# Four of the seven PSUM banks held over the second norm are copied to SBUF in an encoder layer on eight cores

## The reference, cut to what matters

```python
def conv_ffn(x, conv_prev, g_pre, w_up, w_conv, b_conv, w_down, g_post):
    h = rms_norm(x, g_pre)
    gate, val = jnp.split(h @ w_up, 2, axis=-1)          # (B, T, 5632) each
    ext = jnp.concatenate([conv_prev, gate], axis=1)     # two earlier rows in front
    conv = b_conv + sum(ext[:, i:i + T] * w_conv[i] for i in range(3))
    y = (jax.nn.silu(conv) * val) @ w_down
    return rms_norm(y, g_post), ext[:, T:]
```

## Time and profile before

| | us |
|---|---|
| median of 3 runs | 6721.76 |
| lowest and highest run | 6713.4 and 7092.37 |
| the profiled execution's own time | 6715.98 |
| its span on the slowest core (core 4) | 6714.9 |
| spans of the eight cores | 6661.3 to 6714.9 |
| mean granted TensorE clock, core 4 | 0.967 of full |
| TensorE busy | 6102.4 |
| VectorE busy | 2672.6 |
| ScalarE busy | 1740.5 |
| GpSimd busy | 314.4 |

### The profile page before, as it was taken

The page is one execution under the profiler, slowest core; times in us unless marked ns, Lnnn a source line. Parts: engine busy times, 40 slices in busy tenths (PEclk is TensorE's granted clock), DMA queues, the critical chain, the costliest instruction groups (busy, mean ns, idle before and its releaser), DMA issues.

```text
span 6714.9 us, 91958 instructions; the slowest of 8 cores (6661.3 to 6714.9 us)
## 1 busy us (share of the span) xinstructions
PE 6102.4 (91%) x33070; PEld 3235.3 (48%) x33412; DVE 2672.6 (40%) x4680; ACT 1740.5 (26%) x2772; POOL 314.4 (5%) x1160
## 2 busy tenths in 40 slices
PE   6879899898999999899967999899989989998997
PEld 3434345343454445444444455555656565554443
DVE  3343233433334433353333543443444335433532
ACT  2222113221133212331122321321332233223310
POOL 1011000010000000000000100000000000000000
PEclk9989999999999999999988999999999999999999
DMA  9979983899737796444564456457556745754443
GB/s 199 212 152 184 192 218 107 197 207 220 226 120 213 208 244 202 148 163 158 196 217 160 179 197 218 167 205 238 194 186 207 254 159 205 244 197 152 163 158 137
DMA packets 214673, 1276.44 MB, mean 190 GB/s; under 512 B 24192, under 2 KB 45584, under 8 KB 86992
## 3 DMA queue, kind: packets, MB, share of 16 engines
q1 hardware_dynamic: 175376, 1008.93, 43.4%
q0 software_dynamic: 37184, 257.79, 20.7%
q10 hardware_dynamic: 1664, 3.81, 0.2%
HBM read 1275.76 MB, written 184.30 MB: 217 GB/s over the span
## 4 chain that ended last, share of the span: by engine, by line
PE 72%; DMA 15%; DVE 6%; ACT 3%; issue 3%; SPq 0%; DVEq 0%; POOL 0%; ACTq 0%; POOLq 0%
PE ps L533 47%; PE ps L1368 12%; DMA sb_RW<-wall 6%; PE ps L1018 6%; DMA sb_xring<-xt 5%; DMA wb<-sb_RW 2%; PE ps L1260 1%; PE ps L1174 1%; PE ps L644 1%; DVE sb_RB L1237 1%; PE ps L649 1%; PE ps L673 1%; DMA yt<-sb_RB 1%; DMA sb_xring<-cv 1%; DMA sb_RC<-x1d 1%
## 5 line engine op out<-in xcount | busy, mean ns | idle before, releaser
L533 PE MATMUL ps<-sb_RC,sb_RW 128*128 128x512 bf16 (+2 forms) x13530 | 2689.6, 360 | 105.7 <-DMA sb_RW<-wall 51.5
L533 PEld LDWEIGHTS ps<-sb_RC,sb_RW 128*128 128x128 bf16 x13680 | 1340.5, 98 | 1456.1 <-issue 147.9
L1368 PE MATMUL ps<-sb_RA,sb_RW 128*128 128x512 bf16 (+2 forms) x6266 | 1258.3, 362 | 54.9 <-DMA sb_RW<-wall 37.2
L533 PE MATMUL ps<-sb_RD,sb_RW 128*128 128x512 bf16 (+2 forms) x4528 | 1018.7, 372 | 138.0 <-ACT sb_RB L1158 65.9
L1368 PEld LDWEIGHTS ps<-sb_RA,sb_RW 128*128 128x128 bf16 x6336 | 624.3, 99 | 691.2 <-issue 92.1
L533 PEld LDWEIGHTS ps<-sb_RD,sb_RW 128*128 128x128 bf16 x4608 | 450.3, 101 | 583.7 <-issue 231.1
L1305 ACT ACTIVATE sb_RD<-sb_RD,sb_convw 128x512 f32<-128x512 f32 (+2 forms) x440 | 322.4, 733 | 1111.1 <-DVE sb_RD L1295 1036.3
L1295 DVE TENSOR_TENSOR sb_RD<-ps,sb_R 128x512 f32<-128x512 f32 (+1 forms) x378 | 238.7, 631 | 843.6 <-PE ps L533 843.6
L1192 DVE TENSOR_SCALAR sb_RB<-ps,sb_cols 128x512 f32<-128x512 f32 (+2 forms) x288 | 200.9, 698 | 869.1 <-PE ps L1368 473.8
L1018 PE MATMUL ps<-sb_RW,sb_RD 128*128 128x256 bf16 (+1 forms) x4224 | 495.0, 275 | 13.3 <-DMA sb_RW<-wall 7.7
L1308 DVE SCALAR_TENSOR_TENSOR sb_RD<-sb_RD,sb_convw 128x512 f32<-128x512 f32 (+2 forms) x440 | 286.7, 652 | 442.0 <-ACT sb_RD L1305 437.4
(11 more groups left out here) (182 smaller groups left out, 3578.4 us busy)
## 6 DMA issues: line engine op xcount, KB each, us to landing
sb_RW<-wb SPq DMA_DIRECT2D x660, 1024.0 KB, 5.8
sb_RW<-wall POOLq DMA_DIRECT2D x168, 1024.0 KB, 21.6
wb<-sb_RW SPq DMA_DIRECT2D x92, 1024.0 KB, 14.9
sb_RW<-wb SPq DMA_DIRECT2D x55, 768.0 KB, 6.2
sb_xring<-xt SPq DMA_DIRECT2D x64, 512.0 KB, 9.9
sb_RA<-xt SPq DMA_DIRECT2D x24, 1024.0 KB, 14.7
x1d<-sb_RB POOLq DMA_DIRECT2D x20, 1024.0 KB, 4.4
sb_RC<-x1d SPq DMA_DIRECT2D x40, 512.0 KB, 7.4
```

The source lines that it names most:

```text
L533: P(lambda: nc.tensor.matmul(ps[:, 0:nt], lhsT=slab[:, kc, c0:c0 + 128], rhs=rhs[:, kc, 0:nt], start=(kc == 0), stop=(kc == NKC - 1)), rd= ...
L1368: P(lambda: nc.tensor.matmul(ps[:, 0:nt], lhsT=slab[:, kc, c * 128:(c + 1) * 128], rhs=act[:, fc, :], start=(fc == 0), stop=(fc == NFC - 1 ...
```

## The change

A helper `raw(m, bank, eng)` copies a bank as it is into block m of `Yv`, on ScalarE or VectorE, and gives back that block in the bank's place. Right behind `gate_raw(0)` and `gate_raw(1)`, before the norm's matmuls in the program, it is called for the banks of value 0 and value 1 (blocks 0 and 1, ScalarE) and of gate 2 and value 2 (blocks 2 and 3, VectorE). `ffn_gate(2)` and `ffn_value(0)` to `ffn_value(2)` then read these blocks instead of PSUM. Gate 3 and all later chunks stay as they were. Nothing else changes; the order of the banks stays.

```diff
+            def raw(m, bank, eng):
+
+                y = Yv[:, m * nt:(m + 1) * nt]
+                if eng is A:
+                    A(lambda: nc.scalar.copy(out=y, in_=bank[0][:, 0:nt]), rd=[bank[1]], wr=[B_Y[m]])
+                else:
+                    V(lambda: nc.vector.tensor_copy(out=y, in_=bank[0][:, 0:nt]), rd=[bank[1]], wr=[B_Y[m]])
+                return y, B_Y[m]
+
...
             for u in range(2):
                 gate_raw(u, banks[2 * u])
+            held = list(banks)
+            for m, u in enumerate((1, 3, 4, 5)):
+                held[u] = raw(m, banks[u], A if m < 2 else V)
             nxt_v = allb.get()
             rms_from([(accw[:, 0:nt], [B_accw]), (accw[:, nt:2 * nt], [B_accw])], nt, 2, norm_bank)
             fm_chunk(ups[n_first_up][0], ups[n_first_up][1], 128, x1b, B_x1b, nt, nxt_v)
             allb.ids = [allb.ids[1], allb.ids[0]] + allb.ids[2:]
             for u in range(n_first_up):
-                ffn_evac(u, None if u < 2 else banks[2 * u], banks[2 * u + 1])
+                ffn_evac(u, None if u < 2 else held[2 * u], held[2 * u + 1])
             ffn_evac(n_first_up, banks[2 * n_first_up], nxt_v)
```

## The result

| | us |
|---|---|
| before, four runs | 6713.40, 6721.76, 6809.76, 7092.37 |
| changed, four runs | 6673.62, 6679.35, 6681.37, 7334.63 |
| ratio, changed to before, with its 95% interval | 0.9941 [0.9912, 0.997] |
| profiled execution, before and changed | 6715.98 and 6681.37 |

The forecast was 6685. The profiled execution took 34.6 us less than that of before, and the ratio stands for some 40 us (20 to 59, of about 6718).

A forecast was written before the change was run, and what follows sets the result against it. TensorE bounds the kernel, so its stalls and slowed clock matter. Stalls 23.3 plus clock 11.6, less 2.6 and 1.7 in tile 4, give 30.6 us off 6715.98: 6685.4, forecast 6685, range 6670 to 6703.

The forecast's parts named there:

- The wait goes whole: Tiles 3 to 8: TensorE's six waits for the value product on VectorE vanish, 23.3 us gained.
- The clock's 11.6 us: Tiles 3 to 8: TensorE's half clock over the 8 us behind each removed wait goes too, gaining 11.6 us.
- The new wait in tile 4: At tile 4's ninth chunk TensorE waits 2.6 us for value 3's uncopied bank, plus 1.7 us of slow clock.
- Copies at nothing: The four added copies per tile fit idle time on ScalarE and VectorE and cost 0; upper end 10 us.
- The hole: ScalarE's 1.96 us idle before Ln in tile 8, said to hold two copies with 0.9 us left.
- Tiles 0 to 2 at nothing: No gain in tiles 0 to 2: slab loads stay behind gate 3; tile 1's wait grows to 15.7 us.
- Gate 7 of tile 8: Sign in tile 8: this gate starts at VectorE's own pace, about 6 us sooner relative to the norm.
- the sum: Whole kernel: 34.9 us gained less 2.6 and 1.7 in tile 4, 30.6 us net.
- (a): Tiles 3 to 8: only the stall goes, slow clock returns anyway; gain 20.7 us, so 6695; chance 0.12.
- (b): Late slabs 5 to 8, or b3 or b5 still held, take half; gain about 15, 6701; chance 0.08.
- (d): Copies delay R ahead of Ln, holding back all gates; 8 us delay costs 54, so 6739; chance 0.04.
- (c): Tiles 1 and 2 gain too, slab loads finding slots sooner; gain 30.6 + 6.5, so 6679; chance 0.08.

The follow-up runs named there:

- the second group: The changed kernel run again unaltered beside the kernel before: ratio to before 0.9961 [0.994, 0.9982], some 26 us faster.

## Why the prediction was right, and where it wasn't

**The wait goes whole: right.** Tiles 3 and 5 to 8 have none left, and putting that wait alone back restored the time of before.

**The clock's 11.6 us: this is the step that fails.** The term was read from the windows of core 4 alone, taken for every core, and added as a loss that stands by itself behind the wait. Neither holds. In tile 3 of before five of eight cores never left 1.00, and in tile 8 one didn't. And with the wait filled and the clock at 1.00 on all cores, tiles 3 to 8 got back 6.2 us and not 11.6: the second waits, 0.26, 1.70 and 0.47 us, took the place of much of the slow clock. Since the change frees b3, b4 and b5 too, the total didn't suffer, and on core 4, which had been read, the forecast by tile is good: 6.2 us in tile 3, 3.7 in tile 4 and 6.2 in tile 8, forecast 6.1, 3.3 and 6.1.

**Tile by tile** (mean of eight cores, forecast in brackets): tile 3 4.7 us (6.1), tile 4 4.3 (3.3), tiles 5 to 7 5.6, 5.4 and 5.3 (5.0 each), tile 8 5.4 (6.1). The sum is 30.7, forecast 30.6. That it is so close is luck: the terms at 512 columns were too high for the mean core, the narrower ones too low. Where the profiled executions differ by 34.6 us, 33.9 lie in tiles 3 to 8 of core 4 (6.2 each in tiles 3 and 8, 3.7 in tile 4, 17.8 in tiles 5 to 7, of which 2.3 is the wait for the next tile's norm).

**The new wait in tile 4: right.** Forecast 2.6 us at the ninth chunk with 1.7 of clock; measured 2.44, and (1 - 0.79) x 8 = 1.7, on six of eight cores.

**Copies at nothing: right**, with less room than I said. The hole was to keep 0.9 us and kept 0.98 in tile 8, but I had not looked at tile 4, where 0.41 is left. Some 4 us more in front of Ln cost 7 to 13 us in tiles 0 to 2 together, 2.6 in tile 4, 1.3 in each of tiles 5 to 7, and nothing in tiles 3 and 8.

**Tiles 0 to 2 at nothing: right** within what can be told. The wait for `wall` in tile 1 grew to 15.24 us (forecast 15.7). The means of the three tiles together differ by 1.9 us, the two profiles of the changed kernel by 4.6.

**Gate 7 of tile 8** starts 4.7 us sooner behind the norm; I had said about 6. It now stands 3.87 us behind gate 6, so it is VectorE that sets its time, and not TensorE.

**The time itself.** 6685 lay 3.6 us over the profiled execution and at most 11.4 over the two runs beside it. The medians of the four runs each, 6765.76 and 6680.36, lie 85.4 us apart, where the sum says 30.6. It has no term for the rest: two of before's four runs are the 6809.76 and 7092.37 named above, and no run shows the change to have a part in them. The ratio's 40 us and the 26 us of the second group are the better measure, and the forecast 30.6 lies between them and inside both intervals. On the mean core the whole span is 27.8 us shorter than before in the first profile of the changed kernel and 39.6 in the second, so some 10 us outside tiles 3 to 8 play from one execution to the next, and whether the change has a small part in that stays open.

**The rivals.** (a) and (b) fall with the windows and the tile table, (d) with the 0.98 us. (c) falls with tile 2 (0.5 us slower and 0.2 slower in the two profiles, where it asks for 3.2 faster) and with the wait in tile 1; in tile 1 itself the profiles say 1.0 slower and 2.2 faster, which doesn't decide.

## What to carry to other kernels

When a reader of banks is late, count how many banks in a row are late, not only the first: freeing one moved the wait by a chunk and gained nothing, freeing two was nearly enough at 512 columns and not at 448 or 384, and four were enough but for one wait of 2.44 us at 448. A slow clock behind a wait is priced in full only if nothing late stands right behind it; otherwise part of it covers the next wait. Read the clock on all cores and not on the slowest alone: with the same wait, some fall and some don't. And read in-order queues for loads that stand behind small copies: moving such loads ahead was worth about as much again as this change, or a little more.

## What the runs showed of the hardware

The same wait doesn't cost the same clock on each core. In one execution of the kernel before, behind a wait of 3.25 us in tile 8, the mean clock over the next 8 us was 0.64 or 0.65 on four cores, 0.79 or 0.80 on three and 1.00 on one, and the tile took 442.3, 441.1 and 439.9 us; in tile 3 it was 0.64 or 0.65 on three cores and 1.00 on five. The Trainium skill, TensorE: Matmul & The Clock Gate, section "Part 1: The HAM clock gate", says that the point at which the clock changes wanders from run to run; these rows agree, and show it wandering from core to core within one execution too.

A wait filled with needless matmuls kept the clock at 1.00 and yet gave little time: 6.2 us in six tiles, next to nothing in tile 4 (313.9 to 313.7). I hadn't expected that keeping TensorE at full clock could be worth so much less than what the windows behind the wait had shown as lost.
